# Gathering tokens for a pair of experts with two float32r parts of h in place of three bf16 parts

## The reference, cut to what matters

```
scores = sigmoid(xt @ router_w)                    # 256 x 64
idx    = top 8 of the biased scores, within the 4 best of 8 groups
wts    = scores[idx] / sum * 2.5
for each expert e, for the tokens xb that chose it:
    h = silu(xb @ w_gate[e]) * (xb @ w_up[e])      # 1024 -> 256
    y = (h @ w_down[e]) * weight of the token      # 256 -> 1024
routed = sum of y over the experts of a token
shared = (silu(xt @ sw_gate) * (xt @ sw_up)) @ sw_down
out    = layer_norm(ALPHA * x + routed + shared)
```

## Time and profile before

| | |
|---|---|
| runs | 1525.13, 1522.99, 1524.99 us; median 1524.99 |
| profiled execution, first to last instruction | 1523.2 us (no other time of that execution is listed) |
| mean granted clock of TensorE | 0.958 of full speed |
| DMA | 448.84 MB, mean 295 GB/s |
| PE busy | 1434.1 us, 8628 instructions |
| DVE, ACT, POOL busy | 735.8, 227.7, 132.5 us |

### The profile page before, as it was taken

One profiled execution on the slowest core, in us unless ns is written; L12 is line 12 of the kernel. 1 busy time (PEld: TensorE's weight loads), 2 busy tenths in 40 slices (PEclk: granted clock), 3 DMA queues, 4 the chain that ended last, 5 costly groups with the idle time before them and its releaser, 6 DMA issues. The chain is left out here.

```text
span 1523.2 us, 21422 instructions
## 1 busy us (share of the span) xinstructions
PE 1434.1 (94%) x8628; PEld 758.0 (50%) x8628; DVE 735.8 (48%) x1301; ACT 227.7 (15%) x383; POOL 132.5 (9%) x121
## 2 busy tenths in 40 slices
PE   7998999999999999998767988999999999999995
PEld 5763744544544544544443445645444544544542
DVE  3254434444444444444788824344444444444445
ACT  2130211111111111111121022011111111111111
POOL 0000100000000000000777701000000000000000
PEclk9999899999999999999778688999999999999997
DMA  5437579999999999993221038599999999999970
GB/s 173 154 111 304 229 310 369 386 381 376 385 382 379 380 376 384 379 387 139 93 71 67 1 145 335 215 381 372 376 383 378 379 383 380 383 386 371 382 295 28
DMA packets 75545, 448.84 MB, mean 295 GB/s; under 512 B 9457, under 2 KB 10497, under 8 KB 25601
## 3 DMA queue, kind: packets, MB, share of 16 engines
q1 hardware_dynamic: 75520, 448.52, 75.7%
HBM read 447.44 MB, written 1.05 MB: 294 GB/s over the span
## 5 line engine op out<-in xcount | busy, mean ns | idle before, releaser
L945 PE MATMUL bank<-expert_weights,gathered_xT 128*64 128x512 f32 x2048 | 450.4, 592 | 0.0
L945 PEld LDWEIGHTS bank<-expert_weights,gathered_xT 128*64 128x64 f32 x2048 | 146.9, 137 | 292.7 <-issue 292.7
L969 PE MATMUL bank<-expert_weights,hiddenT 128*64 128x512 f32 x1024 | 233.8, 598 | 0.0
L908 PE MATMUL bank<-onehot,weight_ring 128*128 128x128 bf16 x2112 | 201.4, 225 | 0.0
L908 PE MATMUL bank<-onehot,resid 128*128 128x128 bf16 x1056 | 197.0, 224 | 0.0
L893 PE MATMUL bank<-decay_scores,onehotT 128*128 128x512 bf16 x792 | 187.5, 387 | 9.4 <-DVE decay_scores L1642 9.4
L908 PEld LDWEIGHTS bank<-onehot,weight_ring 128*128 128x128 bf16 x2112 | 195.8, 146 | 0.0
L908 PEld LDWEIGHTS bank<-onehot,resid 128*128 128x128 bf16 x1056 | 153.9, 146 | 0.0
L893 PEld LDWEIGHTS bank<-decay_scores,onehotT 128*128 128x128 bf16 x792 | 73.2, 99 | 144.1 <-issue 57.4
L1637 DVE TENSOR_TENSOR expert_out<-expert_out,decay_scores 128x1024 f32<-128x1024 f32 x64 | 78.4, 1225 | 107.1 <-ACT decay_scores L1150 107.1
L969 PEld LDWEIGHTS bank<-expert_weights,hiddenT 128*64 128x64 f32 x1024 | 67.8, 136 | 113.9 <-issue 109.6
(11 more groups left out here) (312 smaller groups left out, 1199.6 us busy)
## 6 DMA issues: line engine op xcount, KB each, us to landing
expert_weights<-in_exp_w_gate SPq DMA_DIRECT2D x128, 1024.0 KB, 8.8
expert_weights<-in_exp_w_up SPq DMA_DIRECT2D x128, 1024.0 KB, 10.8
expert_weights<-in_exp_w_down SPq DMA_DIRECT2D x128, 1024.0 KB, 8.7
weight_ring<-in_w_in_even SPq DMA_DIRECT2D x6, 2048.0 KB, 10.2
weight_ring<-in_w_out SPq DMA_DIRECT2D x4, 2048.0 KB, 7.4
weight_ring<-in_w_in_odd SPq DMA_DIRECT2D x4, 2048.0 KB, 9.7
ln_w<-in_ln_w SPq DMA_DIRECT2D x4, 512.0 KB, 13.2
ln_b<-in_ln_b SPq DMA_DIRECT2D x4, 512.0 KB, 14.3
```

What stands on the lines that cost most here:

```text
L908: last = nc.tensor.matmul(bank[4 + c // 4][:, (c % 4) * P:(c % 4 + 1) * P], h_part[l][i][:, t, :].rearrange("p (q c) -> p c q", c=KC)[:, c ...
L945: last = nc.tensor.matmul(bank[6][a * CAP:(a + 1) * CAP, :].rearrange("p (w f) -> p w f", w=2), xg[:, c, a * CAP:(a + 1) * CAP], ew_gu(2 * ...
L969: last = nc.tensor.matmul(bank[b][a * CAP:(a + 1) * CAP, :], hm[:, j, a * CAP:(a + 1) * CAP], ew_d(2 * u + a)[:, j, half * 512:(half + 1) ...
```

## The change

- `h_top`, a float32r tensor over all of `resid`, takes the first part of h (float32r is a 4-byte type for TensorE; the write rounds). `h_low[l]`, float32r too, takes h minus that, and lies where the second and third bf16 part lay, in the unused half of the ring slot. GpSimd writes it directly, so ScalarE's two casts and VectorE's two subtractions are gone.
- The one-hot is a float32r tensor at the place of the old one (4 bytes an element, all of the 512-float tile).
- The gather has 8 x 2 x 2 = 32 matmuls.
- Since `h_top` fills `resid`, the shared expert's silu and hidden rows move into the first 1024 floats of the ring slot of its gate and up weights, which have been read by then.

```diff
+        def next_offset():
+            return -(-nc.sbuf_base // 32) * 32
...
+        wring_at = next_offset()
         wring = sb("weight_ring", [P, 2, KC * 512])
...
+        resid_at = next_offset()
         resid = sb("resid", [P, TT, D])
...
+        onehot_at = next_offset()
         onehot_f = sb("onehot", [P, 512])
-        onehot = onehot_f[:, 0:2 * TT * CAP].bitcast(BF16).rearrange("p (u t a s) -> p u t a s", u=2, t=TT, a=2)
+        onehot = nc.alloc_sbuf_tensor_at("onehot_r", [P, 2, TT, 2, CAP], FR, offset=onehot_at)
...
-        h_rest = (ysb[:, :], xg[:, :, :].rearrange("p c s -> p (c s)"))
...
-        h_part = [[resid[:, 1, :].bitcast(BF16).rearrange("p (t d) -> p t d", t=TT)] +
-                  [slot_of(f"sh_d{l}")[:, JE * D + i * D:JE * D + (i + 1) * D].bitcast(BF16)
-                   .rearrange("p (t d) -> p t d", t=TT) for i in range(2)]
-                  if f"moe{l}" in stages else None for l in range(2)]
+        h_top = nc.alloc_sbuf_tensor_at("h_top", [P, TT, D], FR, offset=resid_at)
+        h_low = [nc.alloc_sbuf_tensor_at(f"h_low{l}", [P, TT, D], FR,
+                                         offset=wring_at + 4 * (KC * 512 * (ring_no[f"sh_d{l}"] % 2) + JE * D))
+                 if f"moe{l}" in stages else None for l in range(2)]
...
-                nc.gpsimd.tensor_tensor(h_rest[t], h[:, t, :], h_part[l][0][:, t, :], ALU.subtract).then_inc(m["rest"], 1)
+                nc.gpsimd.tensor_tensor(h_low[l][:, t, :], h[:, t, :], h_top[:, t, :], ALU.subtract)\
+                  .then_inc(m["low_part"], 1)
...
                     for t in range(TT):
-                        for i in range(3):
+                        for i, part in enumerate((h_top, h_low[l])):
                             last = nc.tensor.matmul(bank[4 + c // 4][:, (c % 4) * P:(c % 4 + 1) * P],
-                                                    h_part[l][i][:, t, :].rearrange("p (q c) -> p c q", c=KC)[:, c, :],
+                                                    part[:, t, :].rearrange("p (q c) -> p c q", c=KC)[:, c, :],
                                                     onehot[:, par, t, :, :].rearrange("p a s -> p (a s)"),
-                                                    start=(t == 0 and i == 0), stop=(t == TT - 1 and i == 2))
+                                                    start=(t == 0 and i == 0), stop=(t == TT - 1 and i == 1))
...
-        sh_silu = resid[:, 0, :].rearrange("p (w j t) -> p w j t", w=2, j=JE)[:, 0]
-        shid = resid[:, 0, :].rearrange("p (w j t) -> p w j t", w=2, j=JE)[:, 1]
+        sh_silu, shid = ([slot_of(f"sh_gu{l}")[:, w * 512:(w + 1) * 512].rearrange("p (j t) -> p j t", j=JE)
+                          if f"moe{l}" in stages else None for l in range(2)] for w in range(2))
...
-                nc.scalar.copy(h_part[l][0][:, t, :], h[:, t, :]).then_inc(m["top_parts"], 1)
+                nc.scalar.copy(h_top[:, t, :], h[:, t, :]).then_inc(m["top_parts"], 1)
...
-            for t in range(TT):
-                act.wait_ge(m["rest"], t + 1)
-                nc.scalar.copy(h_part[l][1][:, t, :], h_rest[t]).then_inc(m["top_parts"], 1)
...
-            for t in range(TT):
-                dve.wait_ge(m["top_parts"], TT + t + 1)
-                last = nc.vector.tensor_tensor(h_part[l][2][:, t, :], h_rest[t], h_part[l][1][:, t, :], ALU.subtract)
-                last.then_inc(m["low_part"], 1)
-            dve.wait_ge(m["low_part"], TT)
```

More of the change, by code:

```diff
@@ L8 @@
 BF16 = mybir.dt.bfloat16
+FR = mybir.dt.float32r
 I32 = mybir.dt.int32
@@ L178, in build @@
                    "xg_lo xg_hi gu_full silu hidden ht_full ht_ready y_lo_full y_hi_full y_lo y_hi "
-                   "acc_full top_parts rest low_part y_rest y_parts") for l in range(2)]
+                   "acc_full top_parts low_part y_rest y_parts") for l in range(2)]
         M0 = sems("m0_", "params full done_a done_d splus rows em xc lam_exp log_a a_t gain root "
@@ L925, in pe_moe @@
                     for j in range(JE):
-                        last = nc.tensor.matmul(bank[2 * t + n][:, :], shid[:, j, t * P:(t + 1) * P],
+                        last = nc.tensor.matmul(bank[2 * t + n][:, :], shid[l][:, j, t * P:(t + 1) * P],
                                                 wd[:, j, n * 512:(n + 1) * 512], start=(j == 0), stop=False,
@@ L1125, in act_moe @@
                                  ACT.Sigmoid).then_inc(m["scores"], 1)
-            for t in range(TT):
-                act.wait_ge(m["rest"], t + 1)
-                nc.scalar.copy(h_part[l][1][:, t, :], h_rest[t]).then_inc(m["top_parts"], 1)
             act.wait_ge(m["sh_gu"], 1)
-            nc.scalar.activation(sh_silu, bank[0][:, :].rearrange("p (j t) -> p j t", j=JE), ACT.Silu)\
+            nc.scalar.activation(sh_silu[l], bank[0][:, :].rearrange("p (j t) -> p j t", j=JE), ACT.Silu)\
               .then_inc(m["sh_silu"], 1)
@@ L1615, in dve_moe @@
             dve.wait_ge(m["sh_gu"], 2)
-            nc.vector.tensor_tensor(shid, sh_silu, bank[1][:, :].rearrange("p (j t) -> p j t", j=JE), ALU.mult)\
+            nc.vector.tensor_tensor(shid[l], sh_silu[l], bank[1][:, :].rearrange("p (j t) -> p j t", j=JE), ALU.mult)\
               .then_inc(m["sh_hidden"], 1)
```

## The result

The changed kernel takes 2004.35 us (median of 4 runs, 2003.37 to 2006.17) against 1524.61: a ratio of 1.3148, 95% interval 1.313 to 1.3167. It is 480 us slower, where +34 was forecast: slower was right, the size was not. The profiled execution has a span of 2002.8 us.

A forecast was written before the change was run, and what follows sets the result against it. TensorE's closed ring of matmul groups was taken as the bound. 32 matmuls at 110 ns make 3.52 us against 3.0, +0.52 us a gather, x 66 = +34 us on 1523.2, so a 1559 us median; range 1465 to 1600.

The forecast's parts named there:

- What bounds the kernel, and how often: In the expert loop TensorE never rests, so any change to the gather is felt in full, 66 times.
- TensorE's ring of groups: Expert loop, per pair: gate and up, scatter, two short transposes, gather, down, back to gate and up; 16.58 us.
- Bound from below: Gather: float32r matmuls can't be spaced closer than the bf16 ones, 2.89/48 = 60 ns.
- Bound from above: Gather: a float32r matmul costs at most a full f32 product, two instructions of 110 ns, so 220 ns.
- 110 ns for a 4-byte load: Gather: one 4-byte matmul with 128 stationary columns takes 110 ns, 3.52 us against 3.0, +0.52 us a gather.
- The clock: Expert loop: no term for a clock change; a changed length of L969 would mean the working is wrong.
- What hides the rest: Setup before each loop and other work inside it: changes on GpSimd, ScalarE and VectorE are covered, costed at nothing.
- Transfers have room: Expert loop: 16.0 us of DMA work fit in a period of 17.1 us.
- limit of rival A: Expert loop with a 2.02 us gather: transfers need 15.8 us a pair, TensorE 15.5, so 1477 us instead of 1458.
- rival A: Gather: float32r runs at the bf16 spacing, 2.0 us a gather, faster at 1477 us; chance 0.25.
- The gather slows them: 328 GB/s: Expert loop: transfers run at 328 GB/s during a gather, against 392 outside it.
- Rival B: Gather: float32r executes as f32, two instructions or as many passes, 220 ns a matmul, +266 us, 1791 us; chance 0.16.

The follow-up runs named there:

- the float16 kernel: The kernel before with h split into two float16 parts instead of three bf16 ones, float16 one-hot, 32 gather matmuls at the same step of eight elements: 1459.13 us.
- e9_bf16_contiguous: The kernel before with its three bf16 parts read contiguously as stationary operand, features in another order: 1507.72 us.
- e4_contiguous: The changed kernel with the gather's stationary operand read contiguously instead of every eighth float, features in another order: 1563.05 us.
- e13_f32r_permuted: The changed kernel with its float32r parts written with features reordered once per layer, so the gather reads contiguously and stays right: 1561.32 us, ratio 1.0244.
- e11b_data_strided: The changed kernel with the gather's 32 matmuls replaced by 32 f32 transposes of h at a step of 8 floats: 1559.61 us.
- e5_f32_direct: The changed kernel with the gather reading h itself as plain f32, every eighth float, f32 one-hot, no split of h: 1834.82 us.
- e14_ident_strided: The changed kernel with 32 f32 transposes in the gather's place, h read contiguously and the identity at a step of 8 floats: 1823.0 us.

## Why the prediction was wrong, point by point

- **What bounds the kernel, and how often.** Right. TensorE's ring of groups sets the pace before and after, the gather is felt in full, 66 times, and the float16 kernel gains its shorter gathers, 66 us.
- **Bound from below, 60 ns for the bf16 shape.** Held for float32r; for bf16 itself it is no floor, contiguous loads reach 56 (e9_bf16_contiguous).
- **Bound from above, 220 ns.** Failed. I took two f32 records at 110 ns as the worst price of a product. The measured 240 ns is one record, and f32 over the same view takes two of 238, so 476 ns. The bound was built from the shape and the type of the rows and left out how they are read.
- **110 ns for a 4-byte load.** This is the step that failed. Of the three rows behind it L864 and L883 were read rightly, for a stationary operand that lies contiguously: e4_contiguous and e13_f32r_permuted show 110 ns. The third, L849, was to cover the step of eight floats: "Lastly L849 loads h through the very view that the gather uses". It is a transpose, and its price doesn't carry over to a matmul. e11b_data_strided repeats it 32 times at 110 ns, while the same view as stationary operand of a matmul costs 240 ns in float32r and 238 in f32 (e5_f32_direct): +4.7 us a gather instead of +0.5, some 309 us instead of 34. Why a transpose escapes stays open; e14_ident_strided shows only that it pays for its identity's step instead.
- **The clock.** The second step that failed, a term put at nothing. I priced L969 as unchanged, and named a change in its length only as a sign that would make the working wrong. It changed by 166 us: the granted clock fell to 0.50 during the gather and the down matmuls began at that level.
- **What hides the rest.** Right: e13_f32r_permuted has the setup of the change, with its writes reordered, and lies within 3 us of the prediction's 1559. So the sum was right but for the step of the read and what followed from it.
- **Transfers have room.** Right after the change, at 251 to 275 GB/s. As the limit of rival A it was wrong: the float16 kernel came to 1459 us, the time without that limit. "The gather slows them: 328 GB/s" was read from one gather.
- **Rival A** (bf16 spacing) is what a 2-byte type gives. For float32r it did not come: its contiguous matmuls are 110 ns apart, and a load's record lasts 192 ns, as in f32, where contiguous bf16 shows 98 (e9_bf16_contiguous). So the sentence of the Trainium skill that spoke for this rival, that fast weight load is on when the input type is not FP32 (TensorE: Matmul & The Clock Gate, "Weight-path perf modes"), gave float32r no gain here. The estimate of 107 ns for 128 columns from the same page of the Trainium skill agrees with the contiguous 110, and not with the 240 over the step. **Rival B** was wrong as a mechanism: 2112 records, not 4224. Its time of 1791 us came nearer to the measured one than my forecast by luck.

Open: why the clock falls with 128 float32r columns at a spacing of 240 ns and stays with f32 records at nearly the same spacing. The runs show that it does, not why.

## What to carry to other kernels

Price a matmul's weight load by how its operand is read, not by shape and type alone: 4-byte columns 16 or 32 bytes apart cost twice what they cost at 4 or 8 bytes, so reorder such an operand once if it is loaded many times, or see whether it can be the moving one. A transpose is not a sample of a matmul: before resting a sum on a row, ask whether the instruction is of the same kind as the one that you price. And a rate read in one window of one gather is not the rate of all: look at several. And where a group gets slower and sparser on TensorE, look at the granted clock of the group behind it too: here a third of the loss lay in matmuls that nobody had changed.

## What the runs showed of the hardware that I had not expected

- Stationary operand of 128 four-byte columns, spacing of matmuls by step: 110 ns at 1, 116 at 2, 233 at 4, 240 at 8 floats; 64 columns at 8 floats: 122. The 240 ns are the same at a granted clock of 1.00 and of 0.50; the contiguous f32 loads of L864 took 221 ns at 0.50, twice the 110.
- 128 two-byte columns at a step of 8: 62 ns, contiguous: 56, in bf16 and in float16.
- A moving operand of float32r at a step of 8 floats: 111 ns against 110.
- In an f32 transpose the data's step of 8 floats costs nothing (110 ns), and the identity's does: 233 ns, though the load's record then lasts 160 ns and not the 329 or more of a load over the step.
- With 128 float32r columns every 240 ns the granted clock fell to 0.50 in the gather; with 256 columns at 241 ns, f32 records at 238, or f32 transposes at 233 it stayed at 1.00.
- One core's transfers ran at 407 GB/s over 150 us with TensorE fully busy.
